# Attention of the second layer: every second batch of turned groups issues values, turns, scores instead of scores, turns, values

## What is computed

```python
s_c = einsum(q, k_cmp) - slopes * dist_c     # 63 compressed keys
p_c = masked_softmax(s_c);  o_c = p_c @ v_cmp
imp = p_c @ cover;          top = top_k(imp)  # 6 of 16 key blocks
s_s = einsum(q, k_g)  - slopes * dist_s      # the selected blocks
p_s = masked_softmax(s_s);  o_s = p_s @ v_g
s_w = einsum(q, k_blk) - slopes * dist_w     # a window of 512 keys
p_w = masked_softmax(s_w);  o_w = p_w @ v_blk
o = g0 * o_c + g1 * o_s + g2 * o_w
```

## Time and profile before

| | |
|---|---|
| median of three runs | 2946.84 us (2940.65 to 2947.2) |
| profiled execution | 2938.81 us, span of the core 2937.0 us |
| busy of the span | PE 96%, PE weight loads 77%, POOL 55%, DVE 50%, ACT 38% |
| attention of layer 1 with batches | from about 1606 to 2153 us of the span |

### The profile page before, as it was taken

How to read it: one execution, slowest core, us unless ns; L and a number is a source line. 1 busy time by engine, 2 the same in 40 slices (tenths; PEclk the granted TensorE clock), 3 DMA queues, 4 the chain that set the end, 5 groups by cost and what they waited for, 6 DMA issues and landing times.

```text
span 2937.0 us, 43684 instructions
## 1 busy us (share of the span) xinstructions
PE 2820.8 (96%) x16887; PEld 2268.2 (77%) x16887; DVE 1454.0 (50%) x2276; ACT 1117.6 (38%) x1940; POOL 1607.4 (55%) x1194
## 2 busy tenths in 40 slices
PE   6998899999999999999999898999999999999998
PEld 5887877877888888888787666666677888888887
DVE  4555554442955555431401677745526755556325
ACT  3434442331444444100201665677723444443001
POOL 2354524564777776544533555545536777775442
PEclk9999999989999999999999999999999999999999
DMA  4110011122132223421421000000012222224311
GB/s 148 44 30 2 9 37 43 30 72 58 53 91 86 86 86 111 134 77 55 118 72 29 1 1 1 1 1 1 16 30 58 72 86 86 86 77 160 101 51 70
DMA packets 225246, 173.92 MB, mean 59 GB/s; under 512 B 10424, under 2 KB 209597, under 8 KB 224957
## 3 DMA queue, kind: packets, MB, share of 16 engines
q1 hardware_dynamic: 223469, 171.47, 19.0%
q10 hardware_dynamic: 1616, 0.21, 0.0%
HBM read 136.00 MB, written 31.46 MB: 57 GB/s over the span
## 4 chain that ended last, share of the span: by engine, by line
PE 85%; DVE 6%; ACT 4%; POOL 3%; issue 2%; DMA 0%; SPq 0%; DVEq 0%; ACTq 0%; POOLq 0%
PE PS L2377 28%; PE PS L2970 24%; PE PS L3107 4%; PE PS L3128 4%; PE PS L2683 3%; PE PS L3181 3%; PE PS L3147 3%; PE PS L3023 1%; ACT X L1518 1%; PE PS L2525 1%; PE PS L2419 1%; DVE X L1890 1%; PE PS L2508 1%; DVE X L2275 1%; DVE X L1678 1%
## 5 line engine op out<-in xcount | busy, mean ns | idle before, releaser
L636 POOL TENSOR_TENSOR WH<-WR,ONES 128x1024 fp32r<-128x1024 f32 (+1 forms) x108 | 251.6, 2330 | 638.6 <-PE PS L2377 443.2
L642 POOL TENSOR_TENSOR WL<-WR,WH 128x1024 fp32r<-128x1024 f32 (+1 forms) x116 | 286.7, 2471 | 19.2 <-ACT WH L1412 10.4
L965 POOL TENSOR_SCALAR X<-X,STAT,SM 128x640 f32<-128x640 f32 (+6 forms) x215 | 178.5, 839 | 173.4 <-DVE STAT L2286 173.2
L2377 PE MATMUL PS<-YH,WH 128*128 128x512 f32 x864 | 270.1, 394 | 3.3 <-POOL WL L642 2.3
L2377 PE MATMUL PS<-YH,WL 128*128 128x512 f32 x864 | 267.4, 391 | 0.0
L2377 PE MATMUL PS<-YL,WH 128*128 128x512 f32 x864 | 267.3, 391 | 0.0
L2027 DVE SCALAR_TENSOR_TENSOR X<-PS,PTF,X 128x1023 f32<-128x1023 f32 (+1 forms) x176 | 221.4, 1278 | 14.6 <-ACT X L1357 4.3
L1530 ACT ACTIVATE Z<-PS 128x512 f32<-128x512 f32 (+2 forms) x336 | 170.7, 540 | 145.3 <-PE PS L3128 144.0
L2377 PEld LDWEIGHTS PS<-YH,WH 128*128 128x128 f32 x864 | 162.0, 189 | 39.3 <-issue 3.4
L2377 PEld LDWEIGHTS PS<-YH,WL 128*128 128x128 f32 x864 | 163.0, 189 | 34.3
L2377 PEld LDWEIGHTS PS<-YL,WH 128*128 128x128 f32 x864 | 162.8, 188 | 34.2
(11 more groups left out here) (481 smaller groups left out, 6641.0 us busy)
## 6 DMA issues: line engine op xcount, KB each, us to landing
WR<-in_ffn_w_up_dram SPq DMA_DIRECT2D x88, 512.0 KB, 5.0
mid_scratch<-X SPq DMA_DIRECT2D x44, 512.0 KB, 2.6
WR<-in_hy_w_in_dram SPq DMA_DIRECT2D x28, 512.0 KB, 3.9
WR<-in_ffn_w_down_dram SPq DMA_DIRECT2D x32, 448.0 KB, 3.6
X<-mid_scratch SPq DMA_DIRECT2D x28, 512.0 KB, 4.6
Z<-mid_scratch SPq DMA_DIRECT2D x16, 512.0 KB, 7.8
WR<-in_ffn_w_down_dram SPq DMA_DIRECT2D x16, 512.0 KB, 3.8
WR<-in_nsa_w_in_dram SPq DMA_DIRECT2D x14, 512.0 KB, 3.8
```

The costliest lines, as they stand in the source:

```text
L636: pool.tensor_tensor(WH[:, slot, 0:k, :], raw[:, slot, 0:k, :], ONES[:, :].unsqueeze(1).broadcast_to([P, k, P]), ALU.mult).then_inc(w_hi, 1)
L642: pool.tensor_tensor(WL[:, slot, 0:k, :], raw[:, slot, 0:k, :], WH[:, slot, 0:k, :].bitcast(f32), ALU.subtract).then_inc(w_split, 1)
L965: pool.tensor_scalar(score_buf(p, i, 0, w), score_buf(p, i, 0, w), STAT[:, 2, n % 8:n % 8 + 1], GATE[:, qt, gate:gate + 1], ALU.mult, ALU. ...
L2377: ins = pe.matmul(PS[:, bank + 2 * slot + a, :], w[:, slot, i, :], y[:, i, a * HALF:(a + 1) * HALF], start=(nth == 0 and w is WH and y is ...
```

## The change

The three parts of a batch become three local functions, and every second batch calls them in reverse order:

```diff
-                for g in batch:
-                    if g in middle and middle[g] + AHEAD < len(steps):
-                        scores(middle[g] + AHEAD)
-                for g in batch:
-                    if g < pair_groups[-1]:
-                        turn(g)
-                if last_batch - g0 // BATCH < 3:
-                    out_part(0, 2 - (last_batch - g0 // BATCH))
-                for g in batch:
-                    if 0 <= g - LAG < pair_groups[-1]:
-                        values(g - LAG)
+                def scores_part():
+                    ...
+                def turn_part():
+                    ...
+                def value_part():
+                    ...
+                if g0 // BATCH % 2 == 0:
+                    scores_part()
+                    turn_part()
+                    value_part()
+                else:
+                    value_part()
+                    turn_part()
+                    scores_part()
```

More of the change, by code:

```diff
@@ L3187, in _ @@
                 batch = range(g0, g0 + BATCH)
-                for g in batch:
-                    if g in middle and middle[g] + AHEAD < len(steps):
-                        scores(middle[g] + AHEAD)
-                for g in batch:
-                    if g < pair_groups[-1]:
-                        turn(g)
-                if last_batch - g0 // BATCH < 3:
-                    out_part(0, 2 - (last_batch - g0 // BATCH))
-                for g in batch:
-                    if 0 <= g - LAG < pair_groups[-1]:
-                        values(g - LAG)
+                def scores_part():
+                    for g in batch:
+                        if g in middle and middle[g] + AHEAD < len(steps):
+                            scores(middle[g] + AHEAD)
+                def turn_part():
+                    for g in batch:
+                        if g < pair_groups[-1]:
+                            turn(g)
+                    if last_batch - g0 // BATCH < 3:
+                        out_part(0, 2 - (last_batch - g0 // BATCH))
+                def value_part():
+                    for g in batch:
+                        if 0 <= g - LAG < pair_groups[-1]:
+                            values(g - LAG)
+                if g0 // BATCH % 2 == 0:
[6 more added lines that the diff above has]
+                    scores_part()
             for u in range(MT - 1):
```

## The result

| | before | after |
|---|---|---|
| median | 2943.7 us (2940.6 to 2947.2, four runs) | 3077.8 us (3077.2 to 3079.0, four runs) |
| ratio | | 1.0456, 95% interval 1.0438 to 1.0474 |
| span of the profiled execution | 2937.0 us | 3075.4 us |
| attention, from the first turn to the last product with the values | 1606 to 2154 us, 548 | 1604 to 2294 us, 690 |

A forecast was written before the change was run, and what follows sets the result against it. TensorE, busy 96% of the span, was taken as the bound. Terms -24 + 79.5 - 18 + 8 - 5 + 4 = +44.5 us on a 2946.8 us median gave 2991 us, range 2952 to 3050.

The forecast's parts named there:

- Joints: TensorE's switches between part shapes: 142 fewer at 0.17 us each, -24 us, bounds -24 and 0.
- Scores next to scores: 56 odd-to-even joints where scores meet: TensorE waits for VectorE to read each head, +79.5 us, lower bound 40.
- the two terms: TensorE's waits for VectorE: +79.5 us new at the score pairs, -18 us for today's waits, taken as gone.
- Values after values: Odd batch's values wait for ScalarE's copies queued behind exponentials: +29 us, net +8 after today's waits; bounds -20 and +25.
- the term for the turns: Odd batches' scores come 2 us later against their step's turns; waits for GpSimd change by -5 us, bounds -10 and +10.
- The clock: TensorE's granted clock halves after long waits, 3 us a fall; ten falls give 3021 us, thirty 3080; chance 0.18.
- a rival with 0.18: The case that TensorE's clock falls after waits at score pairs, ten of them over 2 us; chance 0.18.
- The upper case of the rival: Thirty falls of TensorE's clock at 3 us each, giving 3080 us; the whole clock case had chance 0.18.
- Output bank and GpSimd: Values waiting for VectorE to free the output bank, +4 us (0 to +16); waits for GpSimd, -5 us (-10 to +10).
- The case "faster": Fewer joints outweigh short waits at score pairs: break-even 0.63 us a pair, 2923 us at 0.2 us; chance 0.07.

The follow-up runs named there:

- Values, scores, turns: Changed kernel with odd batches issuing values, then scores, then turns, so value parts still meet but no two score parts do: 2993.8 us.
- turns, values, scores: Changed kernel with odd batches issuing turns, then values, then scores, so score pairs stay but value parts no longer meet: 3095.9 us.
- sized fillers: Changed kernel plus 3 to 7 unused small TensorE products, by first-step width, before the scores at 31 of 56 score pairs: 3069.8 us.
- the first copy ahead of the exponentials: Changed kernel; where a step starts with a batch's second group, ScalarE copies that group before the exponentials of step p+2: 3035.3 us.

## Why the prediction was wrong

The sign was right, the size a third of what came, and the time outside the range. By its steps:

**Joints: right.** Two value parts in a row now run without one: `2049.05 1.75 PE L3147` has 28 matmuls in one row. 140 joints are gone from the trace, for 142 counted. Their 24 us stay an estimate of 0.17 each; no run shows them by themselves, and the 0.17 is read at joints of turns and values only, while the turns behind the scores at 2005.18 have no such row. They are small beside the rest.

**Scores next to scores: right.** Waits for VectorE rose from 28.5 to 88 us, so by 59.5; the two terms made +61.5. Each held, and not their sum alone: nearly all of the 88 us, about 86, stand at the 56 pairs. The mechanism and its price were in the rows of before, in the reading of 0.82 us and the one place with two score parts. Values, scores, turns confirms it by order alone.

**Values after values: the mechanism right, the term mis-sized by a factor of five.** Waits for ScalarE rose by 41 us where +8 were set. Two things failed. I took the exponentials between two copies at their own length, 1.61 us, as though their input were always there. For five compressed steps it was not: ScalarE stood in front of an exponential whose scores PE had just written, as at 1676.32 above, and PE waited some 3 us each. These five make 15.5 of the 53.5 us; the waits of up to 2.6 us behind ordinary exponentials make the larger part, where the term had 29 us in all. The 3 us are the chain from scores over VectorE and GpSimd to ScalarE, whose length was open to me in the trace of before; I used it for GpSimd alone, in the term for the turns, and not for what else stands in ScalarE's list. And I said that the pairs of scores would give ScalarE time, so that today's waits of 21.5 us go; 18 us, 14 less 0.17 each, stayed at the turns. But the scores that I counted as time given at the odd-to-even joint had been taken from the even-to-odd joint. The order turns, values, scores, with its 64 us at the turns and no value pair, shows that it is this missing cover.

**The clock: the step that failed most.** The forecast had it at zero and left it to a rival with 0.18, priced by ten long falls. The rows of before held what was needed: after one wait of 2.3 us the clock stood at 0.50. I asked which score pairs would wait that long and found ten. Six pairs of that kind (768 keys and more first) do have a fall behind them, as at 1976 above, but of 3.4 us, worth 1.7 where 3 were set. The rest came from places that I did not ask about. Of the ten falls behind standstills of 1.9 us and more, six follow waits for ScalarE at the values (65 us at the lower level), three waits of the turns for GpSimd (31 us) and one a wait for the output bank (24 us), and one of them lasts 27 us. The upper case of the rival, thirty falls and 3080 us, is near the 3078 measured by chance, since half of the loss is not the clock's. Between 22 and 166 us at half clock lie 63 to 72 us, half of the loss; the sized fillers show for a part of them that they hang on PE standing still. A check of the whole account: take from the attention's length the waits that another engine ended (less 0.17 us each), 0.17 us a joint and half of the time at half clock, and 411 us are left for the kernel before, 409 for the changed one and 404 to 430 for the others without fillers, while the lengths themselves run from 538 to 707. With the matmuls' waits for output banks (up to 14.4 us) taken off too, the others have 404 to 416. The Trainium skill, "TensorE: Matmul & The Clock Gate", section "What's actually happening", says that the array's clock is gated by how busy the engine has been of late; the sized fillers agree, with 0.91 against 0.88.

**Output bank and GpSimd: small, as said.** One wait of 2.0 us at the values was for VectorE's output of the step before the last, against +4 set (its own length; the clock fell for 24 us at its end); such waits grew only in kernels that moved ScalarE's work, to 7 to 14 us. Waits of PE's matmuls for GpSimd are 12.5 us after the change; before they were 14.7 (13.5 in the earlier trace rows and 1.2 in a row that is not there), so 2 us went where 5 were set.

The case "faster" had its break-even at 0.63 us a pair; the pairs waited 1.5 us on average in the trace, so it never came near.

## What to carry to other kernels

When two parts of an in-order engine swap places, list for each part what it needs and what it gives cover to: a part that waits for nobody (here the scores between two uses of copies) is worth more in the middle than the joints that a merger saves. Look at the lists of the engines behind as well: a copy that stands behind an instruction whose input comes later than the copy's is late by the whole chain. And where waits add up on TensorE, price them at more than their length, because the work between them may run at the lower clock.

## What the runs showed of the hardware

- A change of TensorE's shape between turns and values costs 0.17 us at the first weight load; at that price the 140 places that went are 24 us, an estimate.
- The granted clock fell to 0.50 behind waits of 1.43 and 0.66 us as well as behind one of 2.85 us; waits of 2.3 us at 1986.97 and 2144.11 have no fall behind them, so the length of one wait does not decide. With waits of 1 to 3 us at every second batch its mean over 690 us was 0.88, down to 0.68 in the 50 us from 1640, where the kernel before had 1.00. More work on TensorE, put into waits, raised it to 0.91 and made the kernel faster.
- The fall feeds on itself only in part: in the second half of the attention, with waits of the same kind, the clock stayed at 0.93 to 0.97. Why the two halves differ is open. The first has the long waits behind compressed steps, but no run took these away alone without moving others.
- A wait that is taken away can uncover another behind it: with the first copy ahead of the exponentials, the waits for ScalarE fell by 43 us, and those of the values for the output bank rose from 2.3 to 11.6.
